# Between the last dense layer and the experts: the router's choice ahead of the norm's root, the first expert's tokens gathered in turned form, and one weight half split early

## The reference, cut to what matters

```python
xp = xp + (u * mixed) @ w_out                 # the output projection, "go" in the kernel
t = rms_norm(x, g)                            # x * rsqrt(mean(x*x) + 1e-6) * g
logits = t @ w_router                         # 8 experts
top_logits, top_idx = lax.top_k(logits, 2)
gates = softmax(top_logits)
combine = sum(one_hot(top_idx, 8) * gates[..., None], axis=1)
for e in range(8):
    out += combine[:, e:e+1] * ((silu(t @ w_gate[e]) * (t @ w_up[e])) @ w_down[e])
```

## Time and profile before

| | us |
|---|---|
| median of 3 runs | 1547.24 (1545.60 to 1547.84) |
| the profiled execution, its own time | 1545.37 |
| its span, first to last instruction | 1543.2 |
| PE busy | 1512.4 |
| DVE busy | 1211.9 |
| ACT busy | 979.4 |
| POOL busy | 166.2 |

### The profile page before, as it was taken

How to read it: one execution, slowest core, us unless ns; L and a number is a source line. 1 busy time by engine, 2 the same in 40 slices (tenths; PEclk the granted TensorE clock), 3 DMA queues, 4 the chain that set the end, 5 groups by cost and what they waited for, 6 DMA issues and landing times.

```text
span 1543.2 us, 21704 instructions
## 1 busy us (share of the span) xinstructions
PE 1512.4 (98%) x8246; PEld 1284.9 (83%) x8246; DVE 1211.9 (79%) x1127; ACT 979.4 (63%) x928; POOL 166.2 (11%) x160
## 2 busy tenths in 40 slices
PE   7899989999999999999999999999999999999998
PEld 5787768999997987888888888888888888888886
DVE  5479774666454958889889889889888888889887
ACT  3343663444344567777777777777777777777774
POOL 2455000000000014801000000000000000100000
PEclk9899999999999999999999999999999999999999
DMA  6346773343655437999999999999999999999990
GB/s 216 117 184 257 277 267 116 127 146 123 234 199 183 168 110 255 380 382 382 393 395 382 393 395 382 394 395 392 384 395 383 381 395 372 378 395 369 375 346 31
DMA packets 199014, 457.30 MB, mean 296 GB/s; under 512 B 12104, under 2 KB 15210, under 8 KB 198954
## 3 DMA queue, kind: packets, MB, share of 16 engines
q1 hardware_dynamic: 190754, 439.27, 76.9%
q0 software_dynamic: 4416, 13.15, 3.0%
q10 hardware_dynamic: 3784, 4.06, 0.8%
HBM read 444.43 MB, written 12.03 MB: 296 GB/s over the span
## 4 chain that ended last, share of the span: by engine, by line
PE 84%; DVE 2%; ACT 1%; issue 0%; DVEq 0%; ACTq 0%
PE bank L1922 18%; PE bank L2377 13%; PE bank L2379 13%; PE bank L2378 13%; PE bank L2391 7%; PE bank L2393 6%; PE bank L2392 6%; PE bank L1909 2%; PE bank L2401 2%; PE bank L2190 1%; PE bank L1917 0%; PE bank L2284 0%; PE bank L2194 0%; DVE ring_r L1348 0%; PE bank L2358 0%
## 5 line engine op out<-in xcount | busy, mean ns | idle before, releaser
L1742 DVE TENSOR_TENSOR wql<-ring,wqh 128x2048 fp32r<-128x2048 f32 x336 | 768.8, 2291 | 108.4 <-ACT wqh L933 107.9
L933 ACT ACTIVATE wqh<-ring 128x2048 fp32r<-128x2048 f32 x336 | 644.9, 1920 | 231.0 <-PE bank L2379 147.8
L2377 PE MATMUL bank<-wqh,xgh 128*128 128x512 f32 x896 | 355.3, 396 | 0.4 <-issue 0.4
L2379 PE MATMUL bank<-wqh,xgl 128*128 128x512 f32 x896 | 349.6, 390 | 0.0
L2378 PE MATMUL bank<-wql,xgh 128*128 128x512 f32 x896 | 349.1, 390 | 0.0
L2379 PEld LDWEIGHTS bank<-wqh,xgl 128*128 128x128 f32 x896 | 168.3, 188 | 36.1
L2377 PEld LDWEIGHTS bank<-wqh,xgh 128*128 128x128 f32 x896 | 168.2, 188 | 34.7 <-issue 0.8
L2378 PEld LDWEIGHTS bank<-wql,xgh 128*128 128x128 f32 x896 | 168.4, 188 | 32.9
L933 ACT ACTIVATE wd<-ring 128x1024 fp32r<-128x1024 f32 x90 | 94.8, 1058 | 129.9 <-PE bank L1922 129.8
L2391 PE MATMUL bank<-wqh,heTh 128*128 128x512 f32 x440 | 171.4, 389 | 0.0
L2393 PE MATMUL bank<-wqh,heTl 128*128 128x512 f32 x440 | 171.2, 389 | 0.0
(11 more groups left out here) (414 smaller groups left out, 2013.7 us busy)
## 6 DMA issues: line engine op xcount, KB each, us to landing
ring<-in_moe_w_gate SPq DMA_DIRECT2D x56, 2048.0 KB, 15.5
ring<-in_moe_w_up SPq DMA_DIRECT2D x56, 2048.0 KB, 15.8
ring<-in_moe_w_down SPq DMA_DIRECT2D x56, 2048.0 KB, 14.9
ring<-in_attn_w_in SPq DMA_DIRECT2D x7, 2048.0 KB, 10.4
ring<-in_ffn_w_gate SPq DMA_DIRECT2D x5, 2048.0 KB, 8.3
ring<-in_ffn_w_up SPq DMA_DIRECT2D x5, 2048.0 KB, 8.0
ring<-in_cache_k SPq DMA_DIRECT2D x16, 512.0 KB, 13.3
ring<-in_cache_v SPq DMA_DIRECT2D x16, 512.0 KB, 5.2
```

Of the source, the lines that this page charges most:

```text
L933: return nc.scalar.activation(dst, src, ACT.Copy)
L1742: return v.tensor_tensor(dst, src, head.bitcast(F32), ALU.subtract)
L2377: mm(bank, xgh[:, k, :], w_h[:, part], start=(k == 0), stop=False)
L2379: last = mm(bank, xgl[:, k, :], w_h[:, part], start=False, stop=(k == KD - 1))
```

## The change

What it does, in order of time:

1. The head and the tail of weight half 0 are made during the output projection, ACT's behind its third group of work there, DVE's behind its fourth residual. The head gets memory of its own, `first_hi`, under buffers that are used later; `squares` moves too.
2. The router's choice is made on the raw logits: the row scale is positive, so the two largest are the same. The sum of squares follows `match_replace`; the root and its reciprocal follow. The softmax gets the scale in ACT's exponential instead, and its inputs are made by POOL, ahead of the empty table.
3. `ho` comes in the order of feature halves, with `pos` (now in a B bank) between the two halves. DVE writes two of the six tails ahead of `pos`, four behind `pick`. The operations on groups 0 and 1 of tokens are joined.
4. `gather_columns` takes the place of `gather_rows`, `turn_rows` and the copy between: the token rows are the stationary operand and `pick` streams, 128 columns at a time, so the result is already turned. 2 x 20 products of 128 columns stand for 2 x 5 of 512 and 8 turns.
5. Both `spare` groups are gone. The first half waits for the first gathered half alone.
6. The exponentials move behind half 4's head on ACT. DVE's loading of `cnt_i` moves behind `combine`.

```diff
@@ scalar, output projection
             heads_before(min(GO0 + m + 1 + WD, GO0 + KD))
+            if m == 2:
+                head(0, 0)
@@ scalar, root and rows
+        act.wait_ge(stored, 16 * N_STORED)
         for t in range(3):
             act.wait_ge(*A.full(("xo", t, 1)))
             half_squares(t, 1)
+        take_xtok(0, 1)
         act.wait_ge(ssum_ok, 1)
         nc.scalar.activation(rtok[:, 0:3], ss[:, 0, 0:3], ACT.Sqrt, ...).then_inc(rroot, 1)
-        for t in range(3):
-            take_xtok(t, 1)
+        take_xtok(1, 1)
         act.wait_ge(rroot, 2)
-        for m in range(3):
-            for half in range(2):
+        for half in range(2):
+            if half:
+                take_xtok(2, 1)
+            for m in range(3):
@@ scalar, gathering and exponentials
-        for n in range(NH):
-            head(0, n)
-        for half in range(2):
-            take_rows(half + 1, banks[6 + half], half)
+        head(0, 1)
         for half in range(2):
             act.wait_ge(ga_full, half + 1)
             take_gathered(banks[6 + half], half)
-        for m in range(3):
-            act.wait_ge(neg_m1, m + 1)
-            nc.scalar.activation(ex[...], ex[...], ACT.Exp, bias=cden[...], accum_out=cden[...])
-        for n in range(NH, HPRO + 3):
+        for n in range(2, HPRO + 3):
             head(0, n)
+            if n == HPRO:
+                act.wait_ge(neg_m1, 1)
+                for m in range(3):
+                    nc.scalar.activation(ex[...], ex[...], ACT.Exp, bias=cden[...],
+                                         scale=rtok[...], accum_out=cden[...]).then_inc(ex_ok, 1)
             if n == HPRO:
                 act.wait_ge(q_used, U0 + 2)
                 silu(0, 0)
@@ vector, output projection
             tails_before(GO0 + min(m + 1 + WD, KD))
+            if m == 3:
+                tail(0, 0)
@@ vector, rows, picks, count
+        rows_tail(0, 0)
+        rows_tail(1, 0)
+        dve.wait_ge(*B.full("pos"))
         ...
         picks(0).then_inc(pick_ok, 1)
+        rows_tail(2, 0)
+        v.tensor_reduce(r8[0:1, 2, 4:5], cnt[0:1, 0:E], AX.X, ALU.max).then_inc(many, 1)
+        rows_tail(0, 1)
         ...
+        rows_tail(1, 1)
         ...
+        rows_tail(2, 1)
@@ vector, gathered
-        tail(0, 0)
-        for half in range(2):
-            gathered_tails(banks[6 + half], half, half + 1)
-        for n in range(1, NH + 1):
-            tail(0, n)
+        gathered_tails(banks[6], 0, 1)
+        tail(0, 1)
+        gathered_tails(banks[7], 1, 2)
+        for n in range(2, HPRO + 3):
+            tail(0, n)
         dve.wait_ge(q_used, U0 + HPRO)
         hidden(0, 0)
+        dve.wait_ge(moe_zero, 3)
         combine()
+        dve.wait_ge(items_ok, 1)
+        last_item = dve.value_load(cnt_i[0:1, 0:1], ...)
@@ tensor
+        def gather_columns(half, bank):
+            for m, low in ((0, 0), (0, 1), (1, 0), (1, 1), (2, 0)):
+                if m == 2 or low:
+                    pe.wait_ge(*A.freed(("ho", m, half)))
+                else:
+                    pe.wait_ge(hoh_ok, 3 * half + m + 1)
+                rows = token_rows(m, low) if m < 2 else htok[:, 4, :]
+                for j in range(4):
+                    c = 4 * half + j
+                    last = mm(bank[:, P * j:P * j + P], rows[:, P * c:P * c + P], pick[:, m, :], ...)
+            last.then_inc(ga_full, 1)
-        spare(A.ap("spare"), pickT[:, 0:P], ysbh[:, 0:CH], 10)
         pe.wait_ge(pick_ok, 1)
         for half in range(2):
-            gather_rows(half, banks[6 + half])
-        for half in range(2):
-            pe.wait_ge(xgr_ok, half + 1)
-            turn_rows(half, banks[6 + half])
-        spare(A.ap("spare"), pickT[:, 0:P], ysbh[:, 0:CH], 5)
-        pe.wait_ge(xg_ok, 2)
+            gather_columns(half, banks[6 + half])
         for n in range(HPRO):
+            if n < 2:
+                pe.wait_ge(xg_ok, n + 1)
             half_tile(0, n, *PRO[n // 2])
```

More of the change, by code:

```diff
@@ L1761, in combine @@
             last.then_inc(comb_ok, 1)
-        dve.wait_ge(*A.full("pos"))
-        v.tensor_copy(cnt[:, 0:E], A.ap("pos")[:, 3 * E:4 * E])
-        v.tensor_copy(pos[:, 0:2, :], A.ap("pos")[:, 0:2 * E].rearrange("p (m e) -> p m e", m=2))
-        v.tensor_copy(pos[0:NS, 2, :], A.ap("pos")[0:NS, 2 * E:3 * E]).then_inc(a_dve, 1)
-        dve.wait_ge(*A.freed("pos"))
-        for m in range(3):
-            r = ROWS[m]
-            last = v.scalar_tensor_tensor(out=pos[0:r, m, :], in0=pos[0:r, m, :], scalar=FAR, in1=sel[0:r, m, :],
-                                          op0=ALU.add, op1=ALU.mult)
@@ L2332, in _ @@
         for m in range(3):
-            for half in range(2):
-                to_tokens(("ho", m, half), uT, m, half, (uT_ok, KD))
-        A.room(pe, "pos")
+            to_tokens(("ho", m, 0), uT, m, 0, (uT_ok, KD))
+        B.room(pe, "pos")
         pe.wait_ge(sel_ok, 1)
@@ L2342, in _ @@
                 left = upper[0:kr, 0:r] if k == m else ones[0:kr, 0:r]
-                last = mm(A.ap("pos")[0:r, E * m:E * m + E], left, sel[0:kr, k, :], start=(k == 0), stop=(k == parts[-1]))
-        last.then_inc(a_full, 1)
-        def gather_rows(half, bank):
-            part = slice(CH * half, CH * half + CH)
-            for m in range(2):
-                for low in range(2):
-                    mm(bank[:], pick[:, m, :], token_rows(m, low)[:, part], start=(m == 0 and low == 0), stop=False)
-            last = mm(bank[:], pick[:, 2, :], htok[:, 4, part], start=False, stop=True)
-            last.then_inc(ro_full, 1)
+                last = mm(B.ap("pos")[0:r, E * m:E * m + E], left, sel[0:kr, k, :], start=(k == 0), stop=(k == parts[-1]))
+        last.then_inc(b_full, 1)
+        for m in range(3):
+            to_tokens(("ho", m, 1), uT, m, 1, (uT_ok, KD))
+        def gather_columns(half, bank):
[7 more added lines that the diff above has]
+                    c = 4 * half + j
+                    last = mm(bank[:, P * j:P * j + P], rows[:, P * c:P * c + P], pick[:, m, :],
+                              start=(m == 0 and low == 0 and j == 0), stop=(m == 2), skip_group_check=True)
+            last.then_inc(ga_full, 1)
         def turn_rows(half, bank):
```

173 lines of the change are left out of this document (88 added, 85 removed).

## The result

The changed kernel takes 1553.03 us (median of 6 runs, 1549.4 to 1558.2), the kernel before 1546.38 beside it: a ratio of 1.0043, 95% interval 1.0029 to 1.0057. I had forecast 1546.0 with a range up to 1550.4.

What follows compares the result with a forecast made beforehand. PE, never pausing in the expert stage, was taken as the bound, so earlier stages' savings arrive one for one. The terms 4.4 - 0.7 - 2.2 - 0.4 = 1.1 us earlier gave a forecast of 1546.0 us, range 1542.5 to 1550.4.

Steps and rivals of the forecast that it cites:

- What bounds the kernel: Expert stage: PE never pauses, so what the stage before saves or loses arrives at the end one for one.
- Choice ahead of the root: Router: choosing on raw logits puts the choice 1.5 us earlier and the picks 3.9 us earlier, at 574.7.
- The gathering: Gathering on PE: 40 products of 128 columns at 0.13 us, 5.2 us; first expert half 4.4 us earlier.
- rival of narrow products at float32's price: Gathering: narrow products cost up to 0.36 us each, making the kernel up to 7.5 us slower, 1554.7; chance 0.08.
- The early split: Output projection: ACT's 1.9 us and DVE's 2.3 us of splitting half 0 hide behind PE; nothing lost.
- The clock: Gathering: a stretch of low PE clock, no longer falling on spares, costs 0.7 us.
- rival of two low stretches: Gathering into half 0: clock stays low through two stretches, 1.6 us slower, 1548.8; chance 0.10.
- The exponentials: ACT between half 4's head and the silu: 2.25 us added, so PE waits 2.2 us for half 5.
- rival "not on the path": ACT's exponentials: half 5 doesn't wait for them, so 3.3 us faster, 1543.9; chance 0.20.
- The register: DVE's load of `cnt_i` between `combine` and half 7's tail: the 0.30 us gap grows by 0.4 us.
- POOL: POOL's chain to item 2's gathered rows: starts later, recovers at line 828; no change taken (-4 to +4.3 us).
- rival "POOL ends last": Item 2's rows: table 4.3 us later, nothing won back, PE waits, net +3.2 us, 1550.4; chance 0.12.

Runs made afterwards that it cites:

- after_second_look: The changed kernel measured once more with nothing altered, for the spread of its wait: 1554.53 us, ratio 1.0048 to the kernel before.
- after_weights_wait: The changed kernel, with SP's first slot-reusing weight tile held until the empty table's four DMAs have landed: 1546.71 us, ratio 1.0005 to the kernel before.
- before_table_late: The kernel before, with 14 small linked memsets on POOL ahead of the empty table's first DMA: 1545.36 us, ratio 0.9997.

## Why the prediction was wrong, step by step

**What bounds the kernel.** Right, and it is why the tables above are so clean: PE hardly pauses between item 1's turn and the last item, and what it has lost or won before arrives there within 0.3 us.

**Choice ahead of the root.** Right: choice +4.83 for a forecast of +4.99, counting done +7.02 for +7.14, picks +8.82 for +8.74.

**The gathering.** Right in kind, 0.5 us too dear: 40 products of 128 columns in 4.66 us, 0.117 each, where I took 0.13 from the turns. The rival of narrow products at float32's price is dead; the nearest rows from below were the right ones. First half at +13.56, 5.15 us earlier instead of 4.4.

**The early split.** Right: the projection's last 48 products take 6.59 us in both kernels.

**The clock.** I took 0.7 us for a low stretch on the gathering. It comes in some executions and not in others: in five of nine profiles of the changed kernel and its variants the router and the gathering ran at 1.00 and the first half came at +13.56 to +13.63; in four the clock was low for a stretch, and it came at +14.34 to +14.40. So the price is 0.8 us and the size was right. These are PE's windows of after_second_look:

```profile
570.00:574.00 4.00, 3.49 (x28) 0.87 0.80 306
574.00:578.00 4.00, 4.00 (x28) 0.70 0.09 4
```

The rule that I weighed in this place (the Trainium skill, "TensorE: Matmul & The Clock Gate", Part 4, turns don't count as busy) would have made the clock low each time, at a cost of 1.7; neither holds. The rival of two low stretches was not seen.

**The exponentials.** Right in size: 2.19 us of PE waiting for a forecast of 2.2. I had put all of it ahead of half 5; 1.17 us of it come one half earlier, since half 4 waits for the silu itself. The rival "not on the path" is dead: taking them off it gave 2.4 us.

**The register.** Right: the gap grew from 0.30 to 0.68 us, 0.38 for a forecast of 0.4.

Up to here the sum would have been 5.15 - 2.2 - 0.4 = 2.6 us, 2.2 by the `he` turns; I had 1.1.

**POOL.** This is the step that failed: "I take no change (-4 to +4.3)", and with it the chance of 0.12 for the rival "POOL ends last". Its start I had right (+8.34 for +8.4, 4.1 late). That this lateness would vanish by the end of line 828 was right too: alone it does, in after_weights_wait (+25.2 against +26.3) and in before_table_late (+26.6). Wrong was that I carried the delay of the first table DMA to the fourth as if the gaps between them were fixed. They are waits for the landing of the DMA ahead, and the earlier half tiles pull the weight tiles into them: the last two take 8.0 and 8.9 us to land in place of 3.7 and 3.4. The fourth lands 13.6 us later than in the kernel before, and the token rows wait for it, a wait that I didn't have at all, so that what line 828 gives back no longer helps. I had even named the earlier weight transfers, as an argument against the rival, for `x_rows`; I hadn't asked what they meet first.

The rival itself named the right place and not the reason: its 4.3 us were the late start, which the runs show to be given back. It was priced at a wait of 4.3 us and 3.2 net; measured were 9.0 of waiting and 2.2 more for the low clock behind it, less the lead of 2.2: 9.1 in the profiled execution. That the chain had only 1.1 us of slack was right, and PE used it up by coming 2.05 us earlier.

## What to carry to other kernels

Before an edit is costed at nothing because it sits on an idle engine, follow the delay to the slack at the far end of that engine's chain, here 1.1 us. POOL's idle gaps between its table DMAs were transfers in flight: when a change makes the consumer earlier, look at which large transfers its freed buffers trigger and what small ones they now meet. And where a late wait takes a gain back, move the wait's place before redoing the gain: one line turned 1553.0 into 1542.7 us.

## What the runs showed of the hardware

A 6 KB DMA issued by POOL landed in 3.5 to 4.1 us in after_weights_wait, where no weight tile was under way, and in 8.0 and 8.9 us beside 2 MB weight tiles in the changed kernel. POOL stood 7.2 to 8.9 us ahead of the fourth one in the five runs with the changed kernel's order on POOL and on SP. In all profiles it started the next table DMA 0.3 to 0.4 us after the one ahead had landed.

POOL's six operations on 8 columns each took 7.68, 5.67, 3.70 and 1.72 us in four executions of nearly the same program, by how much of DVE's weight tails ran beside them: in the execution with 1.72 DVE was idle from 590.4 to 594.4 and the six ran from 592.29 to 594.01. The Trainium skill, "SBUF — State Buffer", SBUF: two separate sides, says that a DVE instruction with two SBUF inputs locks the port pair that it shares with GpSimd, against operations there that read SBUF, for the whole instruction; the trace agrees: a small operation takes 0.2 us, or some 2.2, which is about a tail's 2.29.

The clock of the transition went with the start of the program. In all nine profiles of the changed kernel and its variants, it stayed at 1.00 where the projection ended at 564.89 or earlier, and fell where it ended at 564.93 or later; the kernel before, with its spares, ended at 565.15 or later in four profiles and fell in each. The two sides lie 0.04 us apart, nine executions show this and none was made to test it, so it is a coincidence to look into and no rule; whether the spares do anything stays open. Behind the 9.0 us pause PE ran for some 4 us at 0.50 and lost 2.2 us by it; behind the 3.2 us pause of after_weights_wait 1.6; behind pauses of 0.5 to 0.7 us nothing of the kind was seen.
